# Weight divisions, gate rows and reciprocals rearranged in a one-layer flow-matching kernel

## The reference

```
h = rms_norm(x) * (1 + sc0) + sh0
x = x + 0.5 * g0 * rms_norm((silu(a) * b) @ f_out0)          # a, b = split(h @ f_in0): first FFN
h = rms_norm(x) * (1 + sc1) + sh1
mq, mk, mv, mo, mg, aq, ak, av, bg = split(h @ w_in_mix)
hm = bidirectional mLSTM(mq, mk, mv, gates mg), 8 heads      # gates: scans, exponentials, running maxima
ha = GQA attention(aq, ak, av + cached context), 16 heads    # softmax: exp(s - max) / sum
y = (sigmoid(g_m) * (hm' @ w_bm) + sigmoid(g_a) * (ha @ w_ba)) @ w_out
x = x + g1 * rms_norm(y)
h = rms_norm(x) * (1 + sc2) + sh2
x = x + 0.5 * g2 * rms_norm(second FFN(h))
```

## Time and profile before

| | before |
|---|---|
| median of 3 | 1864.24 us |
| profiled execution | 1866.84 us, span 1865.0 us |
| PE busy | 1797.9 us (96%), mean granted clock 0.984 |
| DVE busy | 979.2 us (53%) |
| ACT busy | 669.4 us (36%) |
| POOL busy | 33.7 us (2%) |
| DMA queue 1 | 176.86 MB, 27.7% of 16 engines |
| `raw` load, issue to landing | 3.4 to 4.0 us |

### The profile page before, as it was taken

One profiled execution on the slowest core, in us unless ns is written; L12 is line 12 of the kernel. 1 busy time (PEld: TensorE's weight loads), 2 busy tenths in 40 slices (PEclk: granted clock), 3 DMA queues, 4 the chain that ended last, 5 costly groups with the idle time before them and its releaser, 6 DMA issues.

```text
span 1865.0 us, 31252 instructions
## 1 busy us (share of the span) xinstructions
PE 1797.9 (96%) x12690; PEld 1732.6 (93%) x12690; DVE 979.2 (53%) x1649; ACT 669.4 (36%) x1159; POOL 33.7 (2%) x40
## 2 busy tenths in 40 slices
PE   7999999999999999999999999989999999999987
PEld 6899999999889998899999898879999999999987
DVE  4866566766367234455537888865372212322334
ACT  3522222212364222534435555533662222221233
POOL 0000000000010000000000000000100000000001
PEclk9999999999999999999999999999999999999998
DMA  7434343432204214232233211102312222222211
GB/s 302 158 147 152 142 154 127 163 136 100 86 14 148 69 69 102 76 92 83 84 129 108 79 38 38 38 30 88 118 52 73 79 68 79 79 68 79 70 54 57
DMA packets 52285, 178.35 MB, mean 96 GB/s; under 512 B 8513, under 2 KB 11091, under 8 KB 51411
## 3 DMA queue, kind: packets, MB, share of 16 engines
q1 hardware_dynamic: 52179, 176.86, 27.7%
HBM read 162.28 MB, written 13.90 MB: 94 GB/s over the span
## 4 chain that ended last, share of the span: by engine, by line
PE 88%; DVE 6%; ACT 4%; issue 1%; DMA 0%; SPq 0%; DVEq 0%; ACTq 0%
PE psum L536 21%; PE psum L537 21%; PE psum L538 21%; PE psum L983 2%; PE psum L993 2%; PE psum L576 2%; PE psum L577 2%; PE psum L578 2%; PE psum L958 2%; PE psum L633 1%; PE psum L875 1%; PE psum L1041 1%; PE psum L1042 1%; PE psum L1043 1%; PE psum L617 1%
## 5 line engine op out<-in xcount | busy, mean ns | idle before, releaser
L536 PE MATMUL psum<-h_hi,whi 128*128 128x320 f32 x2096 | 657.5, 314 | 3.4 <-ACT gate L1349 3.4
L537 PE MATMUL psum<-h_lo,whi 128*128 128x320 f32 x2096 | 649.4, 310 | 0.0
L538 PE MATMUL psum<-h_hi,wlo 128*128 128x320 f32 x2096 | 649.4, 310 | 0.0
L1543 DVE TENSOR_TENSOR wlo<-raw,whi 128x1024 fp32r<-128x1024 f32 x191 | 233.1, 1222 | 610.0 <-ACT whi L1087 610.0
L536 PEld LDWEIGHTS psum<-h_hi,whi 128*128 128x128 f32 x2096 | 395.4, 189 | 10.1 <-issue 6.0
L537 PEld LDWEIGHTS psum<-h_lo,whi 128*128 128x128 f32 x2096 | 395.4, 189 | 1.1
L538 PEld LDWEIGHTS psum<-h_hi,wlo 128*128 128x128 f32 x2096 | 395.2, 189 | 0.0
L1087 ACT CAST whi<-raw 128x1024 fp32r<-128x1024 f32 x191 | 199.3, 1044 | 330.0 <-PE psum L538 315.9
L537 PE MATMUL psum<-g_lo,whi 128*128 128x320 f32 x512 | 158.2, 309 | 0.0
L536 PE MATMUL psum<-g_hi,whi 128*128 128x320 f32 x512 | 158.2, 309 | 0.0
L538 PE MATMUL psum<-g_hi,wlo 128*128 128x320 f32 x512 | 158.2, 309 | 0.0
(11 more groups left out here) (344 smaller groups left out, 2657.1 us busy)
## 6 DMA issues: line engine op xcount, KB each, us to landing
raw<-in_w_ffn_in SPq DMA_DIRECT2D x88, 512.0 KB, 3.5
raw<-in_w_mix SPq DMA_DIRECT2D x77, 512.0 KB, 4.0
mw<-in_w_mod SPq DMA_DIRECT2D x28, 768.0 KB, 5.1
raw<-in_w_ffn_out SPq DMA_DIRECT2D x32, 512.0 KB, 3.4
mw<-in_w_mod SPq DMA_DIRECT2D x4, 2048.0 KB, 19.0
gate<-gate_keep SPq DMA_DIRECT2D x24, 320.0 KB, 4.3
mw<-in_w_mod SPq DMA_DIRECT2D x14, 512.0 KB, 4.1
gate_keep<-gate SPq DMA_DIRECT2D x20, 320.0 KB, 4.6
```

What stands on the lines that cost most here:

```text
L536: mm(out, whi[t.slot][:, k, :], hi[:, k, cols], start=(k == 0), stop=False)
L537: mm(out, whi[t.slot][:, k, :], lo[:, k, cols], start=False, stop=False)
L538: last = mm(out, wlo[t.slot][:, k, :], hi[:, k, cols], start=False, stop=(k == nk - 1))
L1543: tt(lo[:, 0:nk, :], raw[t.raw][:, 0:nk, :], hi[:, 0:nk, :].bitcast(F32), ALU.subtract).then_inc(raw_free, 1)
```

## The change

Six edits, all to the order of work or to where a tile lies:

- In `last_tiles` weights 1 and 2 now lie in the side pairs, 0 and 3 in `whi`/`wlo`, and `SECOND` ends in 0, 3, 1, 2.
- Weight 1 is divided inside the last iteration before `last_tiles`, ahead of that iteration's last product (`last=True`; in the mixer `l == L_OUT - 1`), waiting for no tile. Weight 2 follows directly.
- The table load and the waits for scales come after weight 2. VectorE's `take_mod` and the small scales (`later_scales`) move in front of the last product of the first FFN; `mod_rows` lies elsewhere.
- VectorE's `take(i, 0)` comes before the division of weight i+3; in the second half `take(6, 1)` and `take(7, 1)` come before `first_split(1)` and `(2)`, and `first_split(1)` to `(3)` stand elsewhere on both engines.
- The gate rows' exponentials come one tile later on ScalarE, `turn_gates` and `take_gates` at tile `L_MK + 6`.
- `invert` makes a reciprocal of 2 or 8 columns into `rsum` and copies it out.

```diff
 GROUPS = ((0, slice(0, TP)), (1, slice(TP, N)))
-SECOND = (4, 5, 6, 7, 0, 1, 2, 3)
+SECOND = (4, 5, 6, 7, 0, 3, 1, 2)
...
                    for g in range(2)]
-        mod_rows = at("mod_rows", [MOD_ROWS, MOD_W], F32, mw_at)
+        mod_rows = at("mod_rows", [MOD_ROWS, MOD_W], F32, mw_at + KC * MOD_W * 4)
...
         ko = place("ko", [P, KVH * HD])
+        rsum = place("rsum", [P, 2, 4])
...
         def weights(l, u, base):
-            if u < 2:
+            if u in (0, 3):
                 return whi[(base + u) % 2], wlo[(base + u) % 2]
-            if u < 4:
-                return xhi[u - 2], xlo[u - 2]
+            if u < 3:
+                return xhi[u - 1], xlo[u - 1]
...
+        rs_in = sem("rs_in")
...
                     pe.wait_ge(tr_ev, jb - 1)
-                else:
+                if jb == 6:
...
                 gemm(l)
-                if l == L_MK + 1:
-                    turn_gates()
...
                     turn(l - L_MK - 1)
+                if l == L_MK + 6:
+                    pe.wait_ge(tr_ev, 5)
+                    turn_gates()
...
                 def first_split(u):
...
                     split(Tile(nxt + u), first_weights(u, nxt)[0], Tile(done_by).n + 3)
-                act.wait_ge(mod_mul, 2 * KC * MOD_LATER)
-                if l == 1:
-                    act.wait_ge(misc_st, 16 * 7)
                 split(w[2], weights(l, 2, base)[0], w[0].n + 2, nk)
+                if l != 1:
+                    act.preload_act_table_set(LN_EXP)
+                    act.wait_ge(post_ready, l + 1)
+                    act.wait_ge(mod_ready, 2)
...
                 second(5)
+                high_half(l, 0, range(2, 3))
+                second(6)
                 first_split(1)
-                high_half(l, 0, range(2, 4))
-                second(6)
-                high_half(l, 0, range(4, 6))
+                high_half(l, 0, range(3, 4))
                 second(7)
-                high_half(l, 0, range(6, KC))
+                high_half(l, 0, range(4, 5))
+                first_split(2)
+                high_half(l, 0, range(5, KC))
                 root_y(l, 1)
-                first_split(2)
-                square_x(l, 1, range(0, 3))
+                square_x(l, 1, range(0, 2))
                 first_split(3)
-                square_x(l, 1, range(3, KC))
+                square_x(l, 1, range(2, KC))
...
                 for p, nj in enumerate(PHASES):
-                    def tiles_in(i, past=0, peeled=False, mods=True):
+                    def tiles_in(i, past=0, peeled=False, mods=True, last=False):
...
                                 split(t.plus(4), None, t.n + 3)
+                            elif last and u == 3:
+                                act.wait_ge(mod_mul, 2 * KC * MOD_LATER)
+                                split(t.plus(2), xhi[0], t.n)
...
                         tiles_in(1)
-                        tiles_in(2, mods=False)
+                        tiles_in(2, mods=False, last=True)
+                    elif p == 2:
+                        with act.Fori(0, nj // 2 - 1) as i:
+                            tiles_in(i)
+                        tiles_in(nj // 2 - 1, last=True)
...
                     if p == len(PHASES) - 1:
-                        act.preload_act_table_set(LN_EXP)
-                        act.wait_ge(post_ready, 2 * f + 1)
-                        act.wait_ge(mod_ready, 2)
...
                     fn(t1[:, :, :], t1[:, :, :], ACT.Ln, bias=epsc[0:H, 1:2]).then_inc(row_a, 1)
-                if l == L_MK:
+                if l == L_MK + 1:
...
                     gate_of(KC + l - L_BM)
+                if l == L_OUT - 1:
+                    act.wait_ge(misc_st, 16 * 7)
+                    split(t.plus(2), xhi[0], t.n)
                 done(t)
-                split(t.plus(2))
+                if l < L_OUT - 1:
+                    split(t.plus(2))
...
                 for i in range(KC):
+                    take(i, 0)
...
                         split(w[i + 3], weights(l, i + 3, base), nk)
-                    take(i, 0)
                 take(0, 1)
...
                 take(5, 1)
                 half_normed(l, 0, range(2, 3))
+                take(6, 1)
                 first_split(1)
                 half_normed(l, 0, range(3, 4))
-                take(6, 1)
+                take(7, 1)
                 half_normed(l, 0, range(4, 5))
-                half_normed(l, 0, range(5, 6))
-                take(7, 1)
-                half_normed(l, 0, range(6, KC))
+                first_split(2)
+                half_normed(l, 0, range(5, KC))
                 residual(l, 1, range(0, 3))
-                first_split(2)
-                residual(l, 1, range(3, 6))
                 first_split(3)
-                residual(l, 1, range(6, KC))
+                residual(l, 1, range(3, KC))
...
+            def later_scales():
+                dve.wait_ge(mod_ev, 2)
+                for l in range(3):
+                    scales(l, "post")
+                scales(1, "pre")
+                stt(pre_s[:, 2, :, :], mod[:, 7 * KC:8 * KC, :], 1.0, per_group(V_PRE + 2 * KC),
+                    ALU.add, ALU.mult).then_inc(mod_ready, 1)
+
...
                 for p, nj in enumerate(PHASES):
-                    def tiles_in(i, mods=True, past=0, peeled=False):
+                    def tiles_in(i, mods=True, past=0, peeled=False, last=False):
...
                                 split(t.plus(4))
+                            elif last and u == 3:
+                                split(t.plus(2), (xhi[0], xlo[0]))
+                                if f == 0:
+                                    take_mod()
+                                    later_scales()
...
                         take_rows()
-                        tiles_in(2, False)
-                        take_mod()
+                        tiles_in(2, False, last=True)
+                    elif p == 2:
+                        with dve.Fori(0, nj // 2 - 1) as i:
+                            tiles_in(i)
+                        tiles_in(nj // 2 - 1, last=True)
...
                     if p == len(PHASES) - 1:
-                        if f == 0:
-                            dve.wait_ge(mod_ev, 2)
-                            for l in range(3):
-                                scales(l, "post")
-                            scales(1, "pre")
-                            stt(pre_s[:, 2, :, :], mod[:, 7 * KC:8 * KC, :], 1.0, per_group(V_PRE + 2 * KC),
-                                ALU.add, ALU.mult).then_inc(mod_ready, 1)
...
                     scans(l - 2)
-                if l == L_MK + 1:
-                    take_gates()
...
                     take_turned(l - L_MK - 1)
+                if l == L_MK + 6:
+                    take_gates()
...
                 if ORDER[k][0]:
-                    dve.reciprocal(rb[:, 0:P].rearrange("p (s d) -> p s d", s=2),
-                                   asum[:, :].rearrange("p (s o) -> p s o", o=1).broadcast_to([P, 2, HD])).then_inc(rcp, 1)
-                else:
+                    dve.reciprocal(rsum[:, 0, 0:2], asum[:, :]).then_inc(rs_in, 1)
+                    dve.wait_ge(rs_in, k + 1)
+                    copy(rb[:, 0:P].rearrange("p (s d) -> p s d", s=2),
+                         rsum[:, 0, 0:2].rearrange("p (s o) -> p s o", o=1).broadcast_to([P, 2, HD])).then_inc(rcp, 1)
+                else:
+                    dve.reciprocal(rsum[:, :, :], asum4[:, :, :]).then_inc(rs_in, 1)
+                    dve.wait_ge(rs_in, k + 1)
                     for s in range(2):
-                        last = dve.reciprocal(
-                            rb[:, 0:4 * P].rearrange("p (j s d) -> p j s d", j=4, s=2)[:, :, s, :],
-                            asum4[:, s, :].rearrange("p (j o) -> p j o", o=1).broadcast_to([P, 4, HD]))
+                        last = copy(rb[:, 0:4 * P].rearrange("p (j s d) -> p j s d", j=4, s=2)[:, :, s, :],
+                                    rsum[:, s, :].rearrange("p (j o) -> p j o", o=1).broadcast_to([P, 4, HD]))
...
             def take_second(k):
...
                 g = gate[m]
-                split(t.plus(2))
+                split(t.plus(2), (xhi[0], xlo[0]) if l == L_OUT - 1 else None)
...
```

## The result

The changed kernel took 1843.45 us (median of 4 runs, 1841.23 to 1845.48), the one before 1864.1 (median of 4, 1861.14 to 1864.45): ratio 0.9892, interval 0.9875 to 0.991. The forecast was 1845.2. The profiled execution took 1843.97 us, span 1842.1, so 22.9 us less than the profiled execution before, where the sum of the terms was 19.0.

The account below looks back on a forecast made before the run. TensorE, busy 1797.9 of 1865.0 us, was taken to bound the kernel, leaving 67 us idle and slow-clock losses. 7.0 - 2.4 + 3.6 + 3.5 - 5.3 + 6.5 + 6.1 = 19.0 off 1866.84: 1847.8 profiled, 1845.2 median; range 1838 to 1853.

Parts of the forecast that it names:

- First halves of the FFNs: First eight output tiles at each FFN end: waits on VectorE go, 21.6 us remain; 7.0 and 6.1 us gained.
- its share of 1.7 for the clock: First FFN's end, first half: 1.7 us of the 7.0 gain was put down to the clock.
- Mixer's end, first half: Wait for `a_lo` shrinks as weight 1 is prepared a tile earlier: 2.0 us plus 1.5 of clock, 3.5 gained.
- Gate rows: Transposes and small matmuls run five tiles later, without the exponential wait: 5.3 us gained, 3.6 with one new clock drop.
- Second halves: Ends of first FFN and mixer: the next stage's divisions come later, losing 2.4 and 5.3 us.
- Small reciprocals: Context pairs: narrow reciprocals plus copies gain 0.4 at the first, 4.4 at the last two, 1.7 of clock: 6.5 us.
- the second halves cost nothing: Rival: the new order at the trunk ends loses nothing, 7.7 us better, 1837.5; chance 0.12.
- the clock follows the new gaps: Rival: new waits in second halves and those left at last pairs draw three or four 1.7 us drops, 1851 to 1852; chance 0.2.
- The last weights were never late: Rival judged: late last weights hold up TensorE at three ends, 21 us, 1866 or more; chance 0.02.
- VectorE's waits for the casts: Sign: VectorE waits 2 to 3 us for the cast ahead of the next stage's second and third division.
- TensorE at slice 4: Sign: in the second halves TensorE waits at slice 4; no size given for this wait.
- half clock only near gaps over 2 us: Sign of being right: TensorE's clock falls to half only near gaps over 2 us.

Follow-up runs that it names:

- e4: The changed kernel with VectorE dividing weight i+3 before it takes tile i in the first halves, as in the kernel before: 1850.77 us, ratio 0.9931.
- e7: The kernel before with the small reciprocals alone: 1854.18 us, ratio 0.9953.
- e6: The changed kernel with ScalarE casting weight 1 in the mixer's last iteration only after the last gate tile, as in the kernel before: 1844.71 us, ratio 0.9902.
- e1: The changed kernel with the second halves of the two trunk ends in the order of the kernel before on ScalarE and VectorE: 1833.94 us, ratio 0.9841.
- e2: The changed kernel with the wide reciprocals of the kernel before (128x128 and 128x256, no copy): 1853.57 us, ratio 0.9945.
- e5: The changed kernel with the second halves' old order, weight 2 cast before the root and divided before the residual pass, weight 3 after it: 1829.87 us, ratio 0.9825.
- e10: The changed kernel with a quarter of the reciprocals wide again in the last two pairs: 1848.34 us, ratio 0.9921.
- e11: The changed kernel with half of the reciprocals wide again in the last two pairs: 1845.15 us, ratio 0.9903.

## Why the prediction was right, and where a term was off

**First halves of the FFNs (7.0 and 6.1).** Right: 7.04 and 6.11. e4 splits it: 3.6 the order of take and division, the rest the weights one tile earlier. The length came from counting matmuls (21.6 left, 21.58 measured), so it stands, but its share of 1.7 for the clock was wrong: the drop there cost nothing (e7). The 0.9 by which the first FFN's end was longer than the second's is in two longer waits instead: 1.36 for the last input product and 2.63 on `y`, against 1.02 and 2.05.

**Mixer's end, first half (3.5).** Right at 3.6, by the mechanism shown in e6; 1.4 of it is a half-clock stretch that the wait does not always draw.

**Gate rows (3.6, and 5.3 without a new drop).** Right: 3.4 with the drop that came, 5.0 in e1, e2 and e5 without it. The Trainium skill (TensorE: Matmul & The Clock Gate, Part 4) says that a transpose does not count as busy for the clock in the way of other work; the runs agree only in part, since the block drew the drop in seven traces and none in e1, e2 and e5.

**Second halves (-2.4 and -5.3).** Right, -2.35 and -4.92, and shown by e1. At the first FFN both parts hold too: I had 4.1 lost by waiting and 1.7 won back from the clock. B is 62.61 in e7, with the old order and no drop, so the waiting cost 3.9 and the old drop, which went, gave back 1.5. A new drop did come, behind the wait of 2.49 at 541.61, but it costs nothing (e2). At the mixer's end no drop stands in I in the kernel before, the changed one or e1: all of the 4.92 is waiting.

**Small reciprocals (6.5, bounds 4.8 to 8.2).** This is the term of the sum that was mis-sized: 9.8 in the traces (E and F), 10.1 by the medians of e2. The waiting was close: 0.5 at the first pair (forecast 0.4), 2.58 and 1.83 at the last two (2.2 each). The clock was not: I gave back one slow stretch, 1.7, since 1.1 to 2 us of waiting stay, and 4.9 came back. Both of the last pairs' went (3.2 us: 0.73 and 1.63 draw none, e10 shows one again at 2.37), and the first pair's, for which the sum had no term and which lasted twice as long before, was halved or absent (1.7 in the profile: E 184.9 to 182.7, and 181.1 in five kernels). Why the first pair's came shorter or not at all is open; its wait is 1.79 us with the drop and without.

**The median.** The forecast missed it by 1.8 us while the sum of the terms missed the profile by 3.9. The execution profiled before was one of the longest: over all series that kernel ran between 1860.2 and 1867.2 us (one execution of 4476.7 apart, for which I have no explanation). I took 2.6 off for that on the changed kernel's side too, whose profiled execution lay only 0.5 above its median, and this made up for part of the sum's 3.9. That the median came so close is in part luck.

**Rivals.** That the second halves cost nothing is refuted by e1. That the clock follows the new gaps came true at one place (541.61), where it costs nothing, and one drop stays at the gate rows, which the sum had. The last weights were never late: no wait for a load stands in any of these stretches.

**The signs.** Borne out: the waits on `y` (0.23 us, one per FFN end), none on the last gate product, first halves of 21.6 us, VectorE's waits for the casts (1.5 to 3.4 us, wider than the 2 to 3 that I gave), TensorE at slice 4. Not borne out: half clock only near gaps over 2 us. In the changed kernel a drop stands at the gate rows with no wait ahead of it, one at the first context pair with 1.79, and one here, in D, where the matmul behind a wait of 1.02 takes 0.63 and not 0.31:

```profile
736.21 0.75 PE L864 MATMUL psum<-mq,mk 64*128 64x128 f32 x4 [1.02 <-DVE sa L2011]
736.89 0.63 PE L538 MATMUL psum<-h_hi,whi 128*128 128x320 f32 x1
```

## What to carry to other kernels

In an engine's program order put what frees a buffer (the take) ahead of what prepares a later one (the division), and don't put a step behind a neighbour's cast inside a pass that someone waits for: 3.6 us per FFN end one way, 7.25 the other. Take a reciprocal of the few sums, not of their broadcast. Price a wait of over 2 us at its length plus perhaps one stretch at half clock: 1.5 us where TensorE sets the pace, nothing where it would wait for another engine a little later. At the last two pairs, waits brought down to 0.73 and 1.63 lost both; elsewhere shorter waits kept a drop, so read the granted clock there before counting on it.

## What the runs showed of the hardware that I had not expected

The cost of a reciprocal goes by its output columns: 0.165 us for 2, 0.95 for 128, 1.72 for 256, where a copy of 128 columns within SBUF takes 0.23.

Whether a gap draws half clock is not settled by the gap: the wait of 2.49 at the first FFN's end drew it in seven traces and not in e2, the 2.17 of the old order in three and not in e7. An edit therefore goes with drops of 1.3 to 1.6 us that come or go at places that it does not touch: e1 gained 11.5 us in its profile where its own places account for 7.25, and e11 ran faster than e10 with more work. Medians of small edits carry this; with the span cut into stretches one sees which of them hold a drop.

A slow stretch costs nothing where another engine sets the pace. Two cases stand above, A with and without (31.26 and 31.27) and B of the changed kernel against e2 (66.48 in both). A third: in e6 the granted clock is 0.83 over ten us of the mixer's second half, and 1.00 in the changed kernel, and I is 70.42 and 70.41 us long.

```profile
1350.00:1360.00 10.00, 8.10 (x40) 7.09 (x39) 7.83 (x20) 5.14 (x12) 0.00 (x0) 0.83 0.16 54
```

```profile
1348.00:1358.00 10.00, 7.87 (x47) 6.67 (x46) 7.82 (x20) 5.14 (x12) 0.00 (x0) 1.00 0.16 54
```
